# A scattered row of tiles 2 to 4 scaled and added on GpSimd at the end of layer zero, and the reciprocal of a tile placed behind the next tile's sum

## The reference

```
xp = layer_norm(ALPHA * xp + yp, ln1_g[i], ln1_b[i])
mp = hier_moe(xp, w_group[i], w_expert[i], w_gate[i], w_up[i], w_down[i])
xp = layer_norm(ALPHA * xp + mp, ln2_g[i], ln2_b[i])

def layer_norm(x, g, b):
    mu = mean(x); var = mean((x - mu)**2)
    return (x - mu) * rsqrt(var + LN_EPS) * g + b
```

## Time and profile before

| | |
|---|---|
| time, median of 3 runs | 1390.91 us (1389.66 to 1391.75) |
| the profiled execution | 1391.92 us, its span 1390.0 us |
| instructions | 20247 |
| busy: PE, DVE, ACT, POOL | 1337.8, 543.4, 217.4, 122.2 us |
| HBM traffic | 495.7 MB, 357 GB/s over the span |
| the stage of the change | from 676.95 us (rows back) to 706.79 us (layer one's products) |

### The profile page before, as it was taken

One profiled execution on the slowest core, in us unless ns is written; L12 is line 12 of the kernel. 1 busy time (PEld: TensorE's weight loads), 2 busy tenths in 40 slices (PEclk: granted clock), 3 DMA queues, 4 the chain that ended last, 5 costly groups with the idle time before them and its releaser, 6 DMA issues.

```text
span 1390.0 us, 20247 instructions
## 1 busy us (share of the span) xinstructions
PE 1337.8 (96%) x8652; PEld 892.1 (64%) x8652; DVE 543.4 (39%) x1161; ACT 217.4 (16%) x383; POOL 122.2 (9%) x138
## 2 busy tenths in 40 slices
PE   8999998999999999997899999999999999999896
PEld 7888875656555565664488888666555555566561
DVE  5667765331111211241446878642221111213216
ACT  0000114001000000100134453310000001010012
POOL 0000000111000110121010000010001100111100
PEclk9999999999999999999999999999999999999998
DMA  9700469999999999999992113899999999999995
GB/s 391 294 5 1 171 274 359 405 426 424 427 427 426 427 424 426 425 424 425 373 329 90 61 61 121 303 387 427 426 426 426 426 426 426 425 427 424 424 398 208
DMA packets 67874, 472.48 MB, mean 340 GB/s; under 512 B 16414, under 2 KB 26654, under 8 KB 40127
## 3 DMA queue, kind: packets, MB, share of 16 engines
q1 hardware_dynamic: 51773, 449.37, 78.0%
q0 software_dynamic: 11520, 15.52, 3.2%
q10 hardware_dynamic: 4490, 6.27, 1.5%
HBM read 468.38 MB, written 27.32 MB: 357 GB/s over the span
## 4 chain that ended last, share of the span: by engine, by line
PE 85%; DMA 10%; ACT 2%; DVE 2%; issue 1%; POOL 0%; POOLq 0%; SPq 0%; DVEq 0%
PE ps L1091 27%; PE ps L1127 14%; PE ps L780 10%; PE ps L734 9%; PE ps L824 7%; PE ps L1054 7%; DMA ring<-in_moe_w_up 3%; DMA ring<-in_moe_w_down 3%; PE ps L1041 3%; PE ps L1115 1%; PE ps L1065 1%; PE ps L841 1%; PE ps L1232 1%; DMA ring<-yrows 1%; DMA yrows<-A,Bt 1%
## 5 line engine op out<-in xcount | busy, mean ns | idle before, releaser
L1091 PE MATMUL ps<-ring,A 128*64 128x256 f32 x4096 | 456.1, 379 | 15.7 <-DMA ring<-in_moe_w_up 7.1
L1091 PEld LDWEIGHTS ps<-ring,A 128*64 128x64 f32 x4096 | 326.6, 137 | 155.8 <-issue 39.0
L1127 PE MATMUL ps<-ring,A 128*64 128x512 f32 x1024 | 233.9, 597 | 6.9 <-issue 1.1
L2047 DVE TENSOR_TENSOR A<-A,ps 128x256 f32<-128x256 f32 x64 | 27.0, 421 | 538.4 <-PE ps L1091 538.4
L1127 PEld LDWEIGHTS ps<-ring,A 128*64 128x64 f32 x1024 | 76.0, 136 | 119.2 <-issue 112.7
L734 PE MATMUL ps<-A,ring 128*128 128x260 f32 x576 | 129.6, 387 | 1.3 <-DMA ring<-in_a_w_in 1.3
L734 PEld LDWEIGHTS ps<-A,ring 128*128 128x128 f32 x576 | 110.7, 192 | 18.8 <-DMA ring<-in_a_w_in 1.6
L669 POOL DMA_INDIRECT A<-x,idx x42 | 44.5, 1060 | 673.0 <-PE ps L1041 624.3
L1054 PE MATMUL ps<-C,Bt 104*64 104x512 f32 x400 | 95.7, 620 | 0.0
L2050 DVE COPY A<-ps 128x256 f32<-128x256 f32 x64 | 27.1, 424 | 123.6 <-PE ps L1115 123.6
L1447 ACT ACTIVATE A<-ps 128x512 f32<-128x512 f32 x42 | 25.1, 597 | 305.1 <-PE ps L1127 305.1
(11 more groups left out here) (297 smaller groups left out, 1139.9 us busy)
## 6 DMA issues: line engine op xcount, KB each, us to landing
ring<-in_moe_w_gate SPq DMA_DIRECT2D x62, 2048.0 KB, 23.4
ring<-in_moe_w_up SPq DMA_DIRECT2D x60, 2048.0 KB, 25.0
ring<-in_moe_w_down SPq DMA_DIRECT2D x60, 2048.0 KB, 26.5
ring<-yrows SPq DMA_DIRECT2D x10, 1024.0 KB, 9.8
ring<-in_a_w_in SPq DMA_DIRECT2D x6, 1536.0 KB, 24.7
ring<-in_moe_w_down SPq DMA_DIRECT2D x8, 1024.0 KB, 27.2
ring<-in_b_w_in SPq DMA_DIRECT2D x8, 1024.0 KB, 12.3
ring<-in_moe_w_up SPq DMA_DIRECT2D x6, 1024.0 KB, 43.5
```

The lines of the kernel that those rows point to most:

```text
L1091: mm = pe.matmul(ps[hf * ROWS:(hf + 1) * ROWS, (GATE_BANK, 3)[u], :FH], xgT[:, k, :], ring[:, slot, col:col + FH], start=(k == 0), stop=(k ...
L1127: mm = pe.matmul(ps[nh * ROWS:(nh + 1) * ROWS, 2, :], hidT[:, at:at + ROWS], ring[:, slot, m * D + nh * 512:m * D + (nh + 1) * 512], start ...
L2047: tt(gated, gated, ps[:, 3, :FH], ALU.mult).then_inc(ready, 1)
```

## The change

GpSimd, ahead of `normal(i)`, now scales the k = 1 row of tile i + 2 in place by its weights and adds it to `xk[i + 2]` (two operations of 104x1024, tiles 2 to 4), then signals `row_added`. VectorE no longer does this for these tiles; its sums of tiles 2 to 4 wait for `row_added`. VectorE's `scaling(i)` moves behind `last_expert(i + 1)`, and `into_xT` of a tile stands one place later: behind the sum of tile i + 3, ahead of `scaling(i + 2)`. TensorE adds for tiles 2, 3 and 4 before it turns tile 0. Layer one's orders are the same as before.

```diff
+                def add_row(i, k):
+                    pool.wait_ge(rows_in_sb[i], 16 * (l + 1))
+                    row = picks[l][i][:, k, :]
+                    step(pool.tensor_scalar(row, row, wts[:, k * NT + i:k * NT + i + 1], None, ALU.mult))
+                    pool.tensor_tensor(xk[i], xk[i], row, ALU.add).then_inc(row_added, 1)
...
                 if l == 0:
+                    pool.wait_ge(diag_ok, l + 1)
+                    pool.wait_ge(scaled, l + 1)
                     for i in range(NT):
+                        if i + 2 < NT:
+                            add_row(i + 2, 1)
                         normal(i)
...
-                    for n in ((2, 3) if i == 0 else (i + 3,)):
+                    for n in ((2, 3, 4)[:3 - l] if i == 0 else (i + 3 + (1 - l),)):
...
-                for i in range(NT):
-                    last_expert(i)
-                    if l == 0:
-                        if i + 2 < NT:
-                            chosen(i + 2, 1)
+                if l == 0:
+                    last_expert(0)
+                    for i in range(1, NT):
                         if i >= 2:
-                            into_xT(i - 2)
-                        scaling(i)
-                    else:
+                            dve.wait_ge(row_added, i - 1)
+                        last_expert(i)
+                        if i >= 3:
+                            into_xT(i - 3)
+                        scaling(i - 1)
+                    into_xT(NT - 3)
+                    scaling(NT - 1)
+                    into_xT(NT - 2)
+                    into_xT(NT - 1)
```

More of the change, by code:

```diff
@@ L468, in build @@
         diag_ok = sem("diag_ok")
+        row_added = sem("row_added")
         rows_in_sb = sems("rows_in_sb", NT)
@@ L2167, in _ @@
                 chosen(1, 1)
-                for i in range(NT):
-                    last_expert(i)
-                    if l == 0:
-                        if i + 2 < NT:
-                            chosen(i + 2, 1)
-                        if i >= 2:
-                            into_xT(i - 2)
-                        scaling(i)
-                    else:
+                if l == 0:
+                    last_expert(0)
+                    for i in range(1, NT):
+                        if i >= 2:
+                            dve.wait_ge(row_added, i - 1)
[7 more added lines that the diff above has]
+                    into_xT(NT - 1)
+                else:
+                    for i in range(NT):
+                        last_expert(i)
                         deviation(i)
@@ L2179, in _ @@
                             affine(i - 1)
[L2180 to L2183, removed]
                     affine(NT - 1)
```

## The result

The changed kernel takes 1400.28 us (median of 6 runs, 1398.02 to 1404.83) against 1390.31 (6 runs, 1388.63 to 1391.75): **slower by 0.78%**, ratio 1.0078, 95% interval 1.0066 to 1.0089. The sign was forecast, the size was not: +4.9 us were predicted, +10.0 came, and 1400.28 lies above the range's end of 1398.2.

A forecast was written before the change was run, and what follows sets the result against it. The start of tile 4's transposes, ending layer zero's chain of waits, was taken to bound the kernel. GpSimd's pace and TensorE's fixed tail gave +3.2 us, the clock 1.64: +4.9, so 1395.8 us, range 1391.9 to 1398.2.

The forecast's parts named there:

- The stage: End of layer zero, from TensorE's first scattered-row product to layer one's first product; its delay was to move the whole kernel.
- a scaling is the row of 104x1024 with a per-row scalar: 1.20 us, as `normal`: GpSimd's queue, tiles 2 to 4: each added row's scaling was priced at 1.20 us, taken from `normal`.
- The addition: GpSimd's two-input addition of a row, tiles 2 to 4: 2.39 us as two passes, bounds 1.20 to 3.59.
- The mechanism: End of layer zero: GpSimd busy without a gap to about 702.7, VectorE's sums waiting, TensorE idle about 4 us.
- fixed tail: TensorE behind `normal(2)`, from the third to the last transposes with warming matmuls between: 6.37 us whatever the others do.
- The clock fell: TensorE's granted clock was to fall to 0.50 after a 4 us pause, costing 1.64 us; rival, clock holds: 0.17.
- TensorE's new order decides if the addition is cheap: Rival, chance 0.13: with GpSimd adding at 1.73 us or less, TensorE's back-to-back additions set the pace, +1.3 us, 1392.2.
- The reciprocal behind the next sum: VectorE's reciprocal placed after the next tile's sum: costed at nothing, hidden by the wait for `row_added`.
- The rival of VectorE's held-up products: Chance 0.15: VectorE's small products wait for GpSimd additions, about 0.35 us each, some 0.7 together; +5.6 us, 1396.5.

The follow-up runs named there:

- e8: e1 with 10 more warming matmuls ahead of tile 2's transposes: 1394.08 us, ratio 1.0027 to the kernel before.
- e1: The changed kernel with GpSimd's scaling written with two operations and two per-row scalars, the second a column of ones: 1394.40 us, ratio 1.0025 to the kernel before.
- e2: The kernel before plus five GpSimd operations of 104x1024 ahead of `normal`, four scaling forms and an addition, to time each: 1390.99 us.
- e4: The changed kernel with TensorE's order of before, tile 4's additions behind tile 0's transposes: 1399.02 us, ratio 1.0062 to the kernel before.
- e5: The kernel before with the reorder alone, for tiles 0 to 2; VectorE keeps its rows, GpSimd and TensorE as before: 1389.92 us, ratio 0.9994.

## Why the prediction was wrong

The stage as forecast, and as measured in the changed kernel's second execution, whose tile 2 rows were not late:

```profile
686.97 1.96 PE L1244 MATMUL ps<-ring,Bt 104*104 104x512 f32 x4 [0.72 <-DMA ring<-yrows]
...
689.63 2.84 POOL L729 TENSOR_SCALAR ring<-ring,wts 104x1024 f32<-104x1024 f32 x1 [17.77 <-DMA ring<-yrows]
...
707.74 1.20 POOL L722 TENSOR_SCALAR C<-C,stat 104x1024 f32<-104x1024 f32 x1
...
708.99 1.65 PE L755 MATMUL ps<-ident,C 104*128 104x104 f32 x8 [4.77 <-POOL C L722]
...
716.70 0.88 PE L755 MATMUL ps<-ident,C 104*128 104x104 f32 x8
717.42 1.94 PE L746 MATMUL ps<-A,ring 128*128 128x260 f32 x8
```

| step | forecast, us | measured, us |
|---|---|---|
| stage's start to GpSimd's first operation | 2.5 | 2.66 |
| three rows and three `normal` on GpSimd | 15.1 | 19.31 |
| `normal(2)` to tile 4's transposes, clock up | 6.4 | 6.04 (0.05, and 5.99 as in e8) |
| added by the clock | 1.6 | 1.72 |
| these to layer one's first product | 0.8 | 0.72 |
| sum; more than before | 26.4; +4.9 | 30.45; +8.95 |

- **The step that failed is "a scaling is the row of 104x1024 with a per-row scalar: 1.20 us, as `normal`".** `normal` has two operations and two scalars, the scaling one of each. I took it for a part of `normal`, so at most as dear, and gave it no bounds, while the addition, which looked like the unknown, had them. Three times 1.64 us are 4.9 us, more than this stage's whole miss of 4.05 us. e1 and e2 show it. (The medians miss by 1.0 us more, 10.0 against 4.9; the first execution's stage, 11.66 us longer than before, had 1.55 us of late rows and 1.2 more of the clock. What part such stages have in the timed runs is not shown.)
- The addition: 2.39 us taken, 2.34 measured. The Trainium skill's price of 4497 ns for 2048 columns (GPSIMD Engine Reference, section 3.1), halved to an estimate of 2.25 us, agrees within 4%. GpSimd's wait for itself was 0.08 us (690.89 to 690.97), not the 0.24 us of the program's start, which gave 0.5 us back.
- The mechanism held: GpSimd without a gap, VectorE's sums waiting for it, TensorE pausing ahead of tile 2's transposes (5.48 and 4.77 us where 4 were forecast), the fixed tail behind, and less than a microsecond regained later (683.37 us against 682.40).
- The fixed tail was put 0.4 us too long: 6.37 us from the first to the last transposes held the restart behind each of GpSimd's two waits, which a tail without them does not have (5.99).
- The clock fell, as the forecast assumed; its cost in the stage was 1.7 us (7.71 less 5.99) in one execution and 2.9 (8.89) in the other, 1.64 forecast. What it costs in timed runs stays open: e8 against e1 shows only 0.3 us.
- "TensorE's new order decides if the addition is cheap" was not reached by any run: GpSimd was slower than that in all of them. That the order otherwise brings nothing that can be told is shown by e4.
- The reciprocal behind the next sum was costed at nothing; e5, where it stands so for tiles 0 to 2, is no slower than before.
- The rival of VectorE's held-up products named a real mechanism (below) but not its price: in the changed kernel the two products took 0.55 and 0.67 us instead of 0.16, both during a scaling, and `normal` began as soon as the addition ended. In e8, where two of them met an addition, `normal` began 0.12 us after its end each time, where 0.35 us were put.

## What to carry to other kernels

The price of an instruction with more operations is no upper bound for one with fewer: on GpSimd a multiplication of 104x1024 by one scalar took 2.4 times as long as one by two, so a price is taken from a row of the very form, or bounded on both sides like any unknown, and a neutral second operation may be the cheaper code. Work moved to an idle engine in a chain is paid at that engine's pace for every tile, and what stands fixed behind it, here two batches of warming matmuls, must be held against the gain first: the reorder and the shortening of these were together worth 2.6 us, and moving rows to GpSimd nothing in any of the kernels tried.

## What the runs showed of the hardware

GpSimd's `tensor_scalar` of 104x1024 in float32 takes 2.86 us with one scalar column, 2.77 with one constant, 1.20 with two columns, 1.11 with a column and a constant; its `tensor_tensor` 2.34 to 2.36.

VectorE and GpSimd held each other up where both read two operands from SBUF, and which came second waited. In e8 VectorE's product of two single columns, 0.16 us otherwise, lasted until GpSimd's addition ended:

```profile
689.01 2.35 POOL L731 TENSOR_TENSOR C<-C,ring 104x1024 f32<-104x1024 f32 x1
...
689.85 1.53 DVE L2156 TENSOR_TENSOR stat<-stat 104x1 f32<-104x1 f32 x1
```

In e5 GpSimd's `normal`, with one tensor and its scalars to read, came second to a scattered row on VectorE and took 2.15 us instead of 1.20:

```profile
689.97 1.28 DVE L2163 SCALAR_TENSOR_TENSOR C<-ring,wts,C 104x1024 f32<-104x1024 f32 x1
...
690.17 2.15 POOL L721 TENSOR_SCALAR C<-C,stat 104x1024 f32<-104x1024 f32 x1 [20.98 <-DVE stat L2140]
```

The Trainium skill (SBUF — State Buffer, section "Who interferes with whom") says that VectorE and GpSimd share SBUF ports and that some operations of one hold off the other; this is borne out by these two, with GpSimd needing no second tensor for it. The one-scalar scaling held VectorE off for a part of its time only: there the product lasted 0.55 us and ended 1.12 us after the scaling's start, while 1.7 us of it were still to come. The second product, of 0.67 us, also ended 1.12 us after its scaling's start. Under the two-scalar scaling in e8 the product lasted until the scaling's end (0.88 us, both ending at 693.86).

```profile
688.05 2.84 POOL L729 TENSOR_SCALAR ring<-ring,wts 104x1024 f32<-104x1024 f32 x1 [17.87 <-DMA ring<-yrows]
...
688.62 0.55 DVE L2152 TENSOR_TENSOR stat<-stat 104x1 f32<-104x1 f32 x1
```
